# Four lanes of a differential attention: one step apart, or all on the same step

## The reference, cut to the part that the change touches

The whole program is a two-layer block (feed-forward, RWKV-7 time mix, feed-forward, shared keys and values, feed-forward, differential attention, feed-forward) and then a second block with two more attentions. The change touches the differential attention alone: 8 heads, 512 tokens in 4 query blocks of 128, two softmax maps per head with keys of 64 columns, values of 128 columns.

## Time and profile before

| what | value |
|---|---|
| three runs | 3405.42, 3412.47, 3415.96 us, median 3412.47 us |
| the profiled execution | 3388.53 us, its span 3386.7 us |
| mean granted TensorE clock | 0.949 of full speed |
| busy over the span | PE 3149.7 us (93%), DVE 1666.8 us (49%), ACT 1149.6 us (34%), POOL 142.1 us (4%) |
| the chain that ended last | PE 84%, DVE 9%, ACT 4%, issue 2% |
| the differential attention | from 2135.5 us to 2280.9 us of the span |

### The profile page before, as it was taken

One profiled execution on the slowest core, in us unless ns is written; L12 is line 12 of the kernel. 1 busy time (PEld: TensorE's weight loads), 2 busy tenths in 40 slices (PEclk: granted clock), 3 DMA queues, 4 the chain that ended last, 5 costly groups with the idle time before them and its releaser, 6 DMA issues.

```text
span 3386.7 us, 39065 instructions
## 1 busy us (share of the span) xinstructions
PE 3149.7 (93%) x15716; PEld 2508.4 (74%) x15716; DVE 1666.8 (49%) x2751; ACT 1149.6 (34%) x1853; POOL 142.1 (4%) x145
## 2 busy tenths in 40 slices
PE   7999889899998889999999999769999989988998
PEld 6888567666667768888788888548888767877886
DVE  5434543456655654344754345775535435245235
ACT  4222133344444333223332224453323333233332
POOL 0000000211211100000000000000000000000000
PEclk9999999799999999999999999779999989987999
DMA  4333232000000033333233332003333110201231
GB/s 127 97 96 94 63 111 75 27 28 28 28 28 15 1 118 100 99 94 100 75 100 94 99 97 88 1 22 101 96 94 95 61 38 1 85 13 47 85 96 56
DMA packets 173896, 234.77 MB, mean 69 GB/s; under 512 B 14201, under 2 KB 111062, under 8 KB 173462
## 3 DMA queue, kind: packets, MB, share of 16 engines
q1 hardware_dynamic: 173718, 232.29, 22.1%
HBM read 228.05 MB, written 4.19 MB: 69 GB/s over the span
## 4 chain that ended last, share of the span: by engine, by line
PE 84%; DVE 9%; ACT 4%; issue 2%; POOL 1%; DMA 0%; SPq 0%; DVEq 0%; ACTq 0%
PE banks L830 63%; PE banks L1317 3%; PE banks L972 2%; PE banks L1311 1%; PE banks L963 1%; PE banks L1305 1%; PE banks L1007 1%; PE banks L1034 1%; PE banks L940 1%; PE banks L1030 1%; PE banks L981 1%; DVE diff_scores L2316 1%; DVE diff_small L2322 1%; PE banks L918 1%; ACT L1556 1%
## 5 line engine op out<-in xcount | busy, mean ns | idle before, releaser
L1865 DVE TENSOR_TENSOR weights_lo<-weights_raw,weights_hi 128x1024 fp32r<-128x1024 f32 (+2 forms) x393 | 472.8, 1206 | 1038.2 <-ACT weights_hi L1388 1036.9
L830 PE MATMUL banks<-operand_hi,weights_hi 128*128 128x512 f32 x2208 | 873.0, 395 | 28.3 <-DVE weights_lo L1865 14.5
L830 PE MATMUL banks<-operand_lo,weights_hi 128*128 128x512 f32 x2208 | 865.9, 392 | 0.0
L830 PE MATMUL banks<-operand_hi,weights_lo 128*128 128x512 f32 x2208 | 865.6, 392 | 0.0
L1388 ACT ACTIVATE weights_hi<-weights_raw 128x1024 fp32r<-128x1024 f32 (+2 forms) x393 | 407.9, 1041 | 1090.9 <-PE banks L830 1049.5
L830 PEld LDWEIGHTS banks<-operand_hi,weights_hi 128*128 128x128 f32 x2208 | 418.4, 189 | 123.2 <-issue 25.8
L830 PEld LDWEIGHTS banks<-operand_lo,weights_hi 128*128 128x128 f32 x2208 | 418.9, 190 | 88.6 <-issue 2.2
L830 PEld LDWEIGHTS banks<-operand_hi,weights_lo 128*128 128x128 f32 x2208 | 418.3, 189 | 88.3
L972 PE MATMUL banks<-operand_lo 128*128 128x512 f32 x370 | 173.2, 492 | 1.3 <-ACT v L1508 1.3
L830 PE MATMUL banks<-hidden_ffn_hi,weights_hi 128*128 128x512 f32 x352 | 137.1, 390 | 0.0
L830 PE MATMUL banks<-hidden_ffn_hi,weights_lo 128*128 128x512 f32 x352 | 136.9, 389 | 0.0
(11 more groups left out here) (509 smaller groups left out, 4424.7 us busy)
## 6 DMA issues: line engine op xcount, KB each, us to landing
weights_raw<-in_ffn_w_in_dram SPq DMA_DIRECT2D x352, 256.0 KB, 3.0
weights_raw<-in_ffn_w_out_dram SPq DMA_DIRECT2D x88, 512.0 KB, 3.7
weights_raw<-in_w_in_dram SPq DMA_DIRECT2D x36, 512.0 KB, 3.6
weights_raw<-in_rwkv_w_rkv_dram SPq DMA_DIRECT2D x24, 512.0 KB, 3.8
weights_raw<-in_w_mod_dram SPq DMA_DIRECT2D x24, 512.0 KB, 4.9
weights_raw<-in_w_kv_dram SPq DMA_DIRECT2D x16, 512.0 KB, 3.6
weights_raw<-in_rwkv_w_o_dram SPq DMA_DIRECT2D x8, 512.0 KB, 5.3
weights_raw<-in_diff_w_q_dram SPq DMA_DIRECT2D x8, 512.0 KB, 4.3
```

What stands on the lines that cost most here:

```text
L830: mm = nc.tensor.matmul(o, l, r, start=first and t == 0 and job["opens"], stop=last and t == 2, **skip)
L1865: nc.vector.tensor_tensor(ring_lo[0:p, u["slot"], 0:n, 0:w], ring_raw[0:p, u["ring"], 0:n, 0:w], f32(ring_hi[0:p, u["slot"], 0:n, 0:w]), A ...
```

```
         DIFF_STEPS = 5 * TB + 3
-        DIFF_ORDER = woven(DIFF_HEADS, DIFF_STEPS, LANES, True)
+        DIFF_ORDER = woven(DIFF_HEADS, DIFF_STEPS, LANES, False)
```

## The result

| | kernel before | changed kernel |
|---|---|---|
| median of 20 runs each | 3397.97 us (3382.91 to 3421.27) | 3415.32 us (3403.14 to 3439.95) |
| ratio, 95% interval | | 1.0063 [1.0042, 1.0085] |
| profiled execution | 3388.53 us | 3424.63 us |
| its span, mean granted clock | 3386.7 us, 0.949 | 3422.5 us, 0.941 |
| the differential attention | 145.3 us | 168.9 us |

The changed kernel is slower by 0.63%, 21 us with an interval of 14 to 29; the two medians by themselves differ by 17.4 us.

A forecast was written before the change was run, and what follows sets the result against it. DVE's chain was taken to bound the stage: 50.2 work + 15.0 gaps + 0.6 PE lag + 20.7 tail = 86.5 us a wave, two 173.0 against 145.4. The 27.6 more on 3412.5 gave 3440.1 us, range 3421 to 3455.

The forecast's parts named there:

- DVE's work: In the differential attention, DVE's work for four lanes stays unchanged in kind and takes 50.2 us a wave.
- The gaps: At block borders DVE waits for PE's fourth turn, all lanes' values and a score: 3.3, 5.2, 6.5 us, 15.0 a wave.
- The clock: After pauses, each PE burst starts with the fourth turn at the low clock and reaches the full one 4.6 us in.
- The full clock holds through: Rival: turns during differences keep PE's clock up; gaps 1.9, 3.2, 4.5 us, stage 156.0, total 3423 us; chance 0.13.
- PE behind DVE in block 1: In block 1, two maps at the low clock cost 0.86 us against 0.66 for a lane's biases; 0.6 us a wave.
- Maps side by side: Two score maps run at once on PE's array halves; the rival that they don't gave 3452 us, chance 0.06.
- PE's values hide: Rival: PE does the first lanes' values beside DVE's differences, no gaps; stage 136.8 us, total 3404 us; chance 0.03.
- The exponential's table load: ACT's load of the exponential's table, 1.28 us, is hidden behind DVE's eight maxima in both waves.
- the tail: After a wave's last difference: turn and values 6.4 us, copy 0.4, roots 7.6, scaling to last low operand 6.3; 20.7 in all.
- The median of the runs is 3412.5, and I put the 27.6 on that: Whole program: the stage's 27.6 us increase is added to the known runs' median, giving 3440.1 us.
- time outside the stage: Sign against the forecast: code ahead of and behind the differential attention is the same, so time there should not move.

The follow-up runs named there:

- e_warm_through: Changed kernel with extra overwritten PE matmuls beside DVE's maxima and one behind each of a block's first three turns; stage 155.0 us.
- e_values_ahead: Changed kernel with PE's and ACT's order altered: each lane's values follow the next lane's turn, next scores of all lanes last; stage 156.9 us.
- e_after: Changed kernel run again with no edit; stage 168.8 us, ratio to the kernel before 1.0064.
- e_pairs: Kernel before, with two lanes in step and the other two in step two steps behind (lag of 2); stage 138.6 us, ratio 0.9973.
- e_warm: Changed kernel with extra overwritten PE matmuls beside DVE's maxima only; stage 168.4 us, ratio to the kernel before 1.0111.
- e_scores_ahead: Changed kernel with each lane's values behind the next lane's turn and its next scores right behind its values; stage 171.0 us, ratio 1.0083.
- e_pairs_sq: Kernel before, with lanes in pairs two steps apart and ACT's squares right behind each block's copy; stage 132.4 us, ratio 0.9960.
- e_before_sq: Kernel before, with ACT's squares and sums right behind each block's copy instead of in the tail; stage 145.9 us, ratio 1.0001.
- e_pairs_lag3: Kernel before, with two lanes in step and the other two in step three steps behind; stage 164.8 us.
- e_pairs_lag1: Kernel before, with two lanes in step and the other two in step one step behind; stage 157.7 us.

## Why the prediction was right in kind and too high

Right, step by step:
- **DVE's work.** 50.2 us a wave. The first wave took 2234.77 - 2150.05 = 84.7 us; less gaps of 15.2, a tail of 19.0 and 0.4 of lag it leaves 50.1.
- **The gaps.** All six are there, each released by L1211. Forecast 3.3, 5.2 and 6.5; measured 3.42, 4.92 and 6.88 in the first wave, 3.42, 5.14 and 5.41 in the second. Their sum of 15.0 was met with 15.2 and 14.0.
- **The clock.** 0.50 at each burst's start, as in the earlier trace rows, and up within it. The forecast had it rise 4.6 us in; before block 3 it rose after about 5.3 us in the first wave (0.84 over 2197 to 2198) and after some 2.2 in the second (0.69 over 2278 to 2280), and in the tail of the first wave within some 2 us. So one figure for all bursts was too simple, and that the sum of the gaps was met so closely is in part luck. PE's pauses ahead of the turns were 5.2, 6.2, 8.4 and 10.1 us where the prediction had 4 to nearly 8: it counted the maxima and one difference and not the biases ahead of them. The pace at full clock was right too: `e_warm_through` has the rival's gaps, 1.94, 3.16 and 4.37 against 1.9, 3.2 and 4.5, and its stage of 156.0 as 155.0. "The full clock holds through" was the right sum for a case that doesn't occur by itself.
- **PE behind DVE in block 1.** Forecast 0.6 us; the eight biases took 3.12, and 2.74 in `e_warm_through`: 0.4.
- **Maps side by side.** Eight of width 512 took 3.70 us, four times the pair's 0.86 at the full clock and the drain; in turn they would have taken up to twice that. That rival is out.
- **"PE's values hide"** is out as well: the gaps are there. `e_values_ahead` had to write a part of that case into the list, and its stage was 156.9 us, not 136.8.
- **The exponential's table load** doesn't show in the gaps behind the first maxima, as said.

What was mis-sized in the stage is the term **the tail**: forecast 20.7, measured 19.0 in the first wave and 19.6 in the second. In the first the turn and the values took 5.2 us for 6.4, since the clock rose earlier than 4.6 us in, and the roots 7.3 for 7.6; DVE idled 12.3 and 13.1 us around the roots, where about 14 was forecast. With wave 2's third gap 1.1 below the forecast, the two waves came to 168.9 us for 173.0: 4.1 less.

What put the time outside the range is the step **"The median of the runs is 3412.5, and I put the 27.6 on that"**. The median of 20 runs is 3398.0: the base, taken from three runs, was 14.5 us too high. Two further sets of the kernel before, 25 and 23 runs timed beside the experiments, had medians of 3390.9 and 3403.6. The forecast 3440.1 is 24.8 above the measured 3415.3; 14.5 of it are the base, 4.1 the stage, and 6.2 lie within what two medians of such runs leave open (the interval of the ratio, 14 to 29 us, holds the stage's 23.6). The prediction had a sign before it that was told and not used: the profiled execution was 24 us below that median, in one and the same kernel. The range, 3421 to 3455, was built from the terms of the change alone, with nothing for the base. With the result known one may choose better: on a base half way between the profiled execution and that median, 3400.5, the same terms give 3428 and a range of 3409 to 3443, which holds the time.

It also named time outside the stage as a sign against it. In the profiled execution such time is there, 14.4 us ahead of the stage; `e_after`, with 1.4, shows that it doesn't come from the change.

## What to carry to other kernels

In a pipeline of lanes, look on each engine at what stands directly ahead of the instruction that the busiest engine needs next: if it is work that waits for that engine's last result, the busiest engine idles at each such border, however the lanes are spaced (138.6 us at a lag of 2, 157.7 at 1, 164.8 at 3). Bursts behind an idle TensorE are to be priced at its low clock, but only where something waits for them. And judge an edit of some 20 us in 3400 by the stage it touches, which two executions gave within 0.1 us; whole times of single runs differ by 38 us, and a few of them are no base.

## What the runs showed of the hardware

The stretch from 578 to 1220 us, whose code is the same in all these kernels, was granted another clock in each execution. The windows of it in `e_pairs`, to be held against those above (0.93 before, 0.90 after):

```profile
578.00:1220.00 642.00, 576.05 (x3903) 430.21 (x3901) 349.64 (x774) 255.48 (x486) 118.50 (x121) 0.88 0.07 24
```

The stage's first bias goes with it:

| clock over 578 to 1220 us | first bias of the stage, us |
|---|---|
| 0.93 (before, `e_after`, `e_warm`, `e_values_ahead`) | 2135.6 to 2137.5 |
| 0.91 (`e_scores_ahead`, `e_warm_through`) | 2145.7, 2146.0 |
| 0.90 (changed kernel) | 2150.1 |
| 0.88 or 0.89 (`e_pairs_sq`, `e_before_sq`, `e_pairs_lag3`, `e_pairs_lag1`, `e_pairs`) | 2163.4 to 2172.4 |

That is 36.8 us in the same code, about what the 20 runs of the kernel before spread over (38.4 us). The 20 timed runs of the changed kernel agree: 3403.14 us at a mean clock of 0.947, 3410.9 to 3415.9 at 0.944 to 0.946, 3422 to 3440 at 0.937 to 0.941. Why the clock differs from execution to execution in the same code stays open; no run here was made for it.

Not expected either: the full clock that the extra matmuls of `e_warm` had brought was gone again by the third of four turns, so that a burst right behind them ran at 1.2 GHz; with one matmul more behind each of the first three turns and some more beside the maxima it stayed (`e_warm_through`, 0.94 over the stage). Which of the two additions does it wasn't tested.
